# Forming the remainders of the experts' weights two quarters at a time in a hybrid decoder trunk

## The reference

```
def moe_ffn(xn, router_w, router_b, w1, w3, w2):
    logits = (xn @ router_w).astype(jnp.float32) + router_b.astype(jnp.float32)
    top_v, top_i = lax.top_k(logits, TOP_K)
    ...
    for e in range(N_EXPERTS):
        out = out + gate[..., e:e + 1] * swiglu(xn, w1[e], w3[e], w2[e])
    return out
```

## Time and profile before

| | |
|---|---|
| median of the runs | 1978.64 us |
| the profiled execution | 1977.99 us, of which its span is 1976.1 us |
| TensorE (PE) busy | 1852.5 us, 94% |
| VectorE (DVE) busy | 1488.7 us, 75% |
| ScalarE (ACT) busy | 1191.0 us, 60% |
| mean granted TensorE clock | 0.974 of full speed |
| experts' quarters on VectorE | 672 x 1219 ns |
| the same on ScalarE | 672 x 1054 ns |

### The profile page before, as it was taken

The page is one execution under the profiler, slowest core; times in us unless marked ns, Lnnn a source line. Parts: engine busy times, 40 slices in busy tenths (PEclk is TensorE's granted clock), DMA queues, the critical chain, the costliest instruction groups (busy, mean ns, idle before and its releaser), DMA issues. The chain is left out here.

```text
span 1976.1 us, 29743 instructions
## 1 busy us (share of the span) xinstructions
PE 1852.5 (94%) x10906; PEld 1621.5 (82%) x10907; DVE 1488.7 (75%) x2029; ACT 1191.0 (60%) x1601; POOL 2.4 (0%) x15
## 2 busy tenths in 40 slices
PE   6988898999988989888999999999999999999977
PEld 5866898999987868887888888888888888888867
DVE  7585776555557774947988989889898998988954
ACT  4546643333434558326777777777777777777742
POOL 0000000000000000000000000000000000000000
PEclk8999998999999999988999999999999999999988
DMA  7332352535524323525988989889799898998950
GB/s 287 124 115 111 122 204 113 229 129 219 207 86 147 120 86 129 193 91 201 376 349 342 380 308 384 341 335 385 305 380 373 311 378 307 377 375 310 384 193 22
DMA packets 36789, 485.40 MB, mean 246 GB/s; under 512 B 4048, under 2 KB 6368, under 8 KB 7136
## 3 DMA queue, kind: packets, MB, share of 16 engines
q1 hardware_dynamic: 34272, 481.93, 63.6%
q10 hardware_dynamic: 2432, 2.31, 0.4%
HBM read 483.15 MB, written 1.07 MB: 245 GB/s over the span
## 5 line engine op out<-in xcount | busy, mean ns | idle before, releaser
L1593 DVE TENSOR_TENSOR w_lo<-raw,w_hi 128x1024 fp32r<-128x1024 f32 x672 | 775.8, 1219 | 73.4 <-ACT w_hi L743 72.6
L743 ACT ACTIVATE w_hi<-raw 128x1024 fp32r<-128x1024 f32 x672 | 665.0, 1054 | 104.6 <-DMA raw<-in_moe_w 66.6
L441 DVE TENSOR_TENSOR w_lo<-raw,w_hi 128x1024 fp32r<-128x1024 f32 x236 | 283.8, 1221 | 147.0 <-ACT w_hi L436 140.1
L845 PE MATMUL work<-w_hi,bias_r 128*128 128x512 f32 x896 | 356.8, 398 | 4.3 <-DVE w_lo L1593 4.3
L847 PE MATMUL work<-w_hi,bias_r 128*128 128x512 f32 x896 | 350.3, 391 | 0.0
L845 PE MATMUL work<-x_r,w_hi 128*128 128x256 f32 x1088 | 324.9, 299 | 26.6 <-DVE x_r L1201 16.2
L846 PE MATMUL work<-w_lo,bias_r 128*128 128x512 f32 x896 | 349.9, 390 | 0.0
L846 PE MATMUL work<-x_r,w_hi 128*128 128x256 f32 x1088 | 314.6, 289 | 0.0
L847 PE MATMUL work<-x_r,w_lo 128*128 128x256 f32 x1088 | 314.1, 289 | 0.0
L436 ACT ACTIVATE w_hi<-raw 128x1024 fp32r<-128x1024 f32 x236 | 243.1, 1052 | 107.2 <-PE work L847 55.6
L845 PEld LDWEIGHTS work<-x_r,w_hi 128*128 128x128 f32 x1088 | 215.2, 198 | 38.1 <-issue 30.5
(11 more groups left out here) (270 smaller groups left out, 2290.1 us busy)
## 6 DMA issues: line engine op xcount, KB each, us to landing
raw<-in_moe_w SPq DMA_DIRECT2D x168, 2048.0 KB, 9.7
raw<-in_mix_w SPq DMA_DIRECT2D x34, 2048.0 KB, 8.2
raw<-in_dense_w SPq DMA_DIRECT2D x21, 2048.0 KB, 8.3
raw<-in_ple_w SPq DMA_DIRECT2D x4, 2048.0 KB, 10.8
areaK<-in_ple_p SPq DMA_DIRECT2D x2, 1024.0 KB, 9.5
hT<-in_xT SPq DMA_DIRECT2D x1, 1024.0 KB, 5.4
gate_a<-bias_line ACTq DMA_DIRECT2D x1, 1024.0 KB, 6.8
areaB<-bias_line ACTq DMA_DIRECT2D x1, 1024.0 KB, 9.2
```

What stands on the lines that cost most here:

```text
L441: eng.tensor_tensor(unit(w_lo, g), raw_part(g), unit(w_hi, g).bitcast(F32), ALU.subtract).then_inc(split_ok, 1)
L743: act.activation(w_hi[u][:, :], raw[n % RING][:, (i % 4) * QUARTER:(i % 4 + 1) * QUARTER], ACT.Copy).then_inc(hi_ok, 1)
L845: pe.matmul(out, stat[0], move[0], start=start, stop=False, skip_group_check=True)
L1593: dve.tensor_tensor(w_lo[u][:, :], raw[n % RING][:, (i % 4) * QUARTER:(i % 4 + 1) * QUARTER], w_hi[u][:, :].bitcast(F32), ALU.subtract).th ...
```

## The change

The six places of each ring become slices of one tensor, and VectorE's loop over the 84 quarters of a job becomes one over 42 pairs. One instruction of 128x2048 forms the remainders of quarters i-1 and i. It waits for `hi_ok` of the second of them and raises `split_ok` by 2. A pair never crosses a chunk or the ring's end, since the first of a job has an even place. The work put between quarters stands after odd i in all cases, so its order against the quarters is as before. ScalarE's and TensorE's programs, the DMAs, and the splitting in the mixers, the dense layer and the embeddings (line 441) are as before.

```diff
@@ -194,8 +194,10 @@
         raw = [sb(f"raw{i}", [P, CHUNK]) for i in range(RING)]
-        w_hi = [sb(f"w_hi{i}", [P, QUARTER], F32R) for i in range(UNITS_HELD)]
-        w_lo = [sb(f"w_lo{i}", [P, QUARTER], F32R) for i in range(UNITS_HELD)]
+        hi_ring = sb("w_hi", [P, UNITS_HELD * QUARTER], F32R)
+        lo_ring = sb("w_lo", [P, UNITS_HELD * QUARTER], F32R)
+        w_hi = [hi_ring[:, i * QUARTER:(i + 1) * QUARTER] for i in range(UNITS_HELD)]
+        w_lo = [lo_ring[:, i * QUARTER:(i + 1) * QUARTER] for i in range(UNITS_HELD)]
@@ -1586,15 +1588,16 @@
             def job(j, first):
 
-                def lo_m(i):
+                def lo_pair(i):
                     n = moe_chunk + first * FFN_CHUNKS + i // 4
-                    dve.wait_ge(hi_ok, j * JOB_Q + (4 * moe_chunk + first * JOB_Q + i + 1))
+                    dve.wait_ge(hi_ok, j * JOB_Q + (4 * moe_chunk + first * JOB_Q + i + 2))
                     u = (4 * moe_chunk + i) % UNITS_HELD
-                    dve.tensor_tensor(w_lo[u][:, :], raw[n % RING][:, (i % 4) * QUARTER:(i % 4 + 1) * QUARTER],
-                                      w_hi[u][:, :].bitcast(F32), ALU.subtract).then_inc(split_ok, 1)
-
-                for i in range(JOB_Q):
-                    lo_m(i)
+                    at_ring = slice(u * QUARTER, (u + 2) * QUARTER)
+                    dve.tensor_tensor(lo_ring[:, at_ring], raw[n % RING][:, (i % 4) * QUARTER:(i % 4 + 2) * QUARTER],
+                                      hi_ring[:, at_ring].bitcast(F32), ALU.subtract).then_inc(split_ok, 2)
+
+                for i in range(1, JOB_Q, 2):
+                    lo_pair(i - 1)
                     if i == 3 + AHEAD:
                         add_combined(j + first)
```

## The result

The changed kernel takes 2017.62 us (median of four runs, 2017.14 to 2018.33) against 1977.81 for the kernel before beside it: 1.020 times, interval 1.0183 to 1.0218, or 39.8 us more. The forecast was slower by 20.3 us, 1999, with a range up to 2013. The direction was right, and the size was half of what came.

What follows compares the result with a forecast made beforehand. TensorE was taken as the bound, VectorE's saving costed at 0. Later remainders add 15.7 us in jobs 1 to 7, 3.4 in job 0 and 1.2 for late landings, 20.3 in all: 1999 us, range 1991 to 2013.

Steps and rivals of the forecast that it cites:

- The pair's duration: One subtraction of 2048 columns on VectorE takes 2.28 us, with bounds of 1.22 and 2.44.
- The pair's start: VectorE starts a pair 0.03 us after the second copy ends; usable 4.37 us after the first copy's start.
- Head of a job: Jobs 1 to 7: quarter 0 stalls TensorE 0.99 us, within the combine's additions moving 0.80 later; cost 0.80 each.
- quarter 10: Its remainder now waits for quarter 11's copy, which stands behind ScalarE's wait for the turned gates; 1.15 us a job.
- The w2 chunks: At quarters 28, 40, 52, 64 and 76 the pair is just late: 0.05 us each, 0.25 a job.
- Quarter 16: After VectorE's stretch without idle time, the pair (16, 17) is usable just after TensorE comes; 0.04 us a job.
- Late landings: Chunks going from landing to copy to remainder without pause lack 3.8 us of lead; a third taken, 1.2 us.
- Job 0: TensorE's wait for the first remainder is 2.0 us longer; 3.4 with the other terms, half clock taken at 0.
- VectorE as the pace: Rival: VectorE sets the pace, so the 27 us saved come out in full, 1952; 2 in 100.
- the quick pair: Rival: 2048 columns take little more than 1024, making good the later start; 1977.7 at 1.22 us; 4 in 100.
- The ring as the bound: Rival: reissuing into the ring of three chunks takes longer than TensorE's three chunks; 24 us, 2023; 9 in 100.
- The clock: Rival: a new stall in each job brings 4.7 us at half clock, 2.4 us a job, 2018; 4 in 100.

Runs made afterwards that it cites:

- x_w2single: Changed kernel, but the first pair at quarters 28, 40, 52, 64 and 76 is two instructions of one quarter; 2003.04 us, ratio 1.0135.
- the two cuts: Changed kernel, but the first instruction at quarters 28, 40, 52, 64 and 76 covers 1920 or 1792 columns, not 2048; 2010.33 and 2007.88 us.
- x_hi_first: Changed kernel, but TensorE runs a quarter's four matmuls that read w_hi first, the two that read w_lo last; 1996.12 us, ratio 1.0082.
- x_five_places: Changed kernel, but two single instructions replace the pair at quarters 0, 10, 16, 28, 40, 52, 64 and 76; 1993.66 us, ratio 1.008.

## Why the prediction was wrong

- *What bounds it*: right. TensorE had nothing to win, VectorE's saving of 19 us (27 forecast) came to nothing, and the pair's readiness was what counted.
- *The pair's duration*, 2.28 us: measured 2.287.
- *The pair's start*: taken at 0.03 us after the second copy, as for one quarter; measured 0.10. The lead that a pair needs is 4.46 us, not 4.37.
- *Head of a job and quarter 10*: right in place and in the main size. The head cost 0.88 for 0.80, but by another sum: the stop at quarter 0 costs 1.25 (0.99 forecast) and the combine's wait of 0.36 goes. Quarter 10 cost 1.37 for 1.15.
- *The w2 chunks*: this step failed. I wrote "Cost 0.05, at quarters 28, 40, 52, 64 and 76: 0.25", and that the lead was used up to the last tenth. Each cost 0.3, forty times, which makes 12 us against 2. Quarter 16 is the same, 0.33 for 0.04, eight times 2.3 us more. Of the 0.24 us missed at a w2 chunk some 0.08 are lateness of the matmul itself (0.13 in place of 0.05), nearly all of it the pair's later start, and some 0.16 are lost in the matmuls behind. For those I had a term of 0: I had compared the remainder with the start of the matmul, and took from the start of job 0, where TensorE had stood still for 4.32 us, that it starts 0.06 after the remainder, which it does, and goes on at its pace from there, which it doesn't. The weight load, which in the running kernel starts 0.22 ahead, waits for the same semaphore. x_w2single, the two cuts and x_hi_first show the size; that the load behind the wait is the cause rests on the rows of the loads and on the table of seven places, in two of which the matmul is on time, not on a run that frees the load alone.
- *Late landings*: 1.2 us forecast, 0.8 measured. The third that I took was a guess. The reason given, that the stops ahead give the landings room, fits x_five_places, where most of the stops are gone and late remainders cost 5.2.
- *Job 0*: 2.0 for the first wait, measured 2.1; the half clock, taken at 0, cost 0.7.
- *After the loop*: not foreseen at all, 2.0 to 4.8 us. It has nothing to do with the mechanism forecast.
- *The miss in sum*, from the table: of the 20 us between the forecast and the first profile the w2 chunks are 10, quarter 16 2.3, quarter 10 1.8, the heads 0.6, job 0's clock and the later start of the loop 1.5, after the loop 4.8. The w2 chunks alone would have left the time inside the range, at 2009.
- *The rivals*: VectorE as the pace and the quick pair didn't come. The ring as the bound didn't either: a landing takes 9.6 us (9.7 before) and ScalarE's wait for it is unchanged. The clock held at 1.00 in jobs 1 to 7 through all stops of 1 us.

The Trainium skill says that where VectorE isn't saturated but causes gaps on other engines, breaking up its instructions may let work be done sooner (page "Perfetto Trace Analysis", section "Optimizing Scalar/DVE Operations"). The traces agree: with the joined instructions VectorE's idle time before them rose by 76 us while the kernel lost 40, and two single ones in place of the first at five places of a job (x_w2single) gave back 14.6.

## What to carry to other kernels

An operand is due when TensorE's weight load would start, not when its matmul would: here a matmul late by 0.13 us cost 0.3, one on time behind a late load still 0.09, and the matmul's rows showed next to nothing of it, so look at the rows of the weight loads. See too how many steps the waiting instruction raises: here raising by 2 made it start 0.07 us later. Joining small instructions of an engine that isn't the bound makes the first result later by the joined length and by the wait for the last input; count the leads at every place of the loop, and where the stops go, count again, since stops hide other lateness. If a product is made of several passes, run those first whose operands come first: it gave back 21 of 40 us here.

## What the runs showed that I had not expected

- A matmul that starts on time can still cost TensorE 0.09 us, when its weight load was 0.18 late.
- An instruction of VectorE that raises a semaphore by 2 starts 0.10 us after the copy that it waits for, one that raises it by 1 0.03. Only instructions of 2048 columns raise by 2 here, but one of 1920 columns starts after 0.03.
- VectorE's first branch past a spare job took 0.5 us in before and 2.8 in the changed kernel, and the DMA behind it says the same of all others: 2.8 or 5.2 us, never between. The kernel with the wait of a pair but single instructions has 5.1.
- Behind the loop the time follows the granted clock as well: two profiles of the changed kernel, with the same branch, differ by 2.7 us there at means of 0.79 and 0.83.
- Moving four additions by two quarters saves 4 us of 1978, more than the 2.7 us of waits that the profile showed.
